# First slabs of a two-block transformer kernel: order of the first loads, gate logits as rounded products, and GpSimd's place in the opening

## The reference

```python
def hybrid_mixer(h, w_in, forget_b, ret_norm_g, w_out, valid):
    proj = jnp.einsum('bld,de->ble', h, w_in)
    rq, rk, rv, rg, fq, fk, fv, ff = jnp.split(proj, SPLIT_POINTS, axis=-1)
    o_r = retention(...)
    ...
    log_f = jax.nn.log_sigmoid(ff.astype(jnp.float32) + forget_b.astype(jnp.float32))
    o_f = forgetting_attention(fq..., fk..., fv..., log_f, valid)
    mixed = jnp.concatenate([o_r, o_f], axis=-1).astype(h.dtype)
    return jnp.einsum('ble,ed->bld', mixed, w_out)

def forgetting_attention(q, k, v, log_f, valid):
    c = jnp.cumsum(log_f, axis=1)           # logits get c[t] - c[s]
    ...
```

## Time and profile before

| | |
|---|---|
| median of 3 runs | 1465.71 us (1465.19 to 1465.89) |
| the profiled execution | 1465.56 us, span of the core 1463.8 us |
| TensorE busy | 1456.0 us, 99% of the span |
| VectorE / ScalarE / GpSimd busy | 902.1 / 768.0 / 490.2 us |
| HBM read | 247.79 MB |

### The profile page before, as it was taken

How to read it: one execution, slowest core, us unless ns; L and a number is a source line. 1 busy time by engine, 2 the same in 40 slices (tenths; PEclk the granted TensorE clock), 3 DMA queues, 4 the chain that set the end, 5 groups by cost and what they waited for, 6 DMA issues and landing times.

```text
span 1463.8 us, 30914 instructions
## 1 busy us (share of the span) xinstructions
PE 1456.0 (99%) x11461; PEld 1422.5 (97%) x11461; DVE 902.1 (62%) x1572; ACT 768.0 (52%) x1096; POOL 490.2 (33%) x209
## 2 busy tenths in 40 slices
PE   9999999999999999999999999999999999999998
PEld 7999999989999999999999999999999999999987
DVE  7437888755445369989644434544447898864533
ACT  6456655555445445567544534444444657654443
POOL 5541000443334303710244442443420570044442
PEclk9999999999999999999999999999999999999999
DMA  7435566655556545445555654555544535567763
GB/s 267 127 95 169 172 189 193 216 165 158 175 172 208 167 129 169 141 150 165 179 172 172 209 179 127 186 170 183 203 151 144 173 119 184 174 195 201 207 190 112
DMA packets 75882, 250.92 MB, mean 171 GB/s; under 512 B 15776, under 2 KB 18208, under 8 KB 75808
## 3 DMA queue, kind: packets, MB, share of 16 engines
q1 hardware_dynamic: 75280, 249.65, 54.6%
q10 hardware_dynamic: 528, 0.26, 0.1%
HBM read 247.79 MB, written 1.05 MB: 170 GB/s over the span
## 4 chain that ended last, share of the span: by engine, by line
PE 97%; DVE 1%; POOL 1%; issue 0%; DMA 0%; ACT 0%; SPq 0%; POOLq 0%; DVEq 0%
PE W L1645 27%; PE W L1646 27%; PE W L1647 27%; PE W L1733 3%; PE XP L1797 2%; PE XQ L1797 1%; PE W L1732 1%; PE W L1697 1%; PE W L1748 1%; PE W L1747 1%; PE W L1698 1%; PE W L1746 1%; PE W L1699 1%; DMA raw<-in_w 0%; POOL wlo L455 0%
## 5 line engine op out<-in xcount | busy, mean ns | idle before, releaser
L455 POOL TENSOR_TENSOR wlo<-raw,whi 128x1024 fp32r<-128x1024 f32 (+1 forms) x184 | 470.7, 2563 | 924.8 <-ACT whi L518 924.8
L1645 PE MATMUL W<-xh,whi 128*128 128x272 f32 (+2 forms) x2400 | 689.8, 287 | 0.2 <-POOL wlo L455 0.2
L1646 PE MATMUL W<-xl,whi 128*128 128x272 f32 (+2 forms) x2400 | 687.0, 286 | 0.0
L1647 PE MATMUL W<-xh,wlo 128*128 128x272 f32 (+2 forms) x2400 | 685.9, 286 | 0.0
L518 ACT ACTIVATE whi<-raw 128x1024 fp32r<-128x1024 f32 (+1 forms) x440 | 481.1, 1098 | 136.0 <-PE W L1647 94.1
L1645 PEld LDWEIGHTS W<-xh,whi 128*128 128x128 f32 x2400 | 452.4, 188 | 2.7 <-issue 1.5
L1647 PEld LDWEIGHTS W<-xh,wlo 128*128 128x128 f32 x2400 | 452.2, 188 | 0.0
L1646 PEld LDWEIGHTS W<-xl,whi 128*128 128x128 f32 x2400 | 451.3, 188 | 0.2
L986 DVE TENSOR_TENSOR wlo<-raw,whi 128x1024 fp32r<-128x1024 f32 (+1 forms) x255 | 331.9, 1302 | 80.1 <-ACT whi L518 79.7
L1645 PE MATMUL W<-ax,whi 128*128 128x272 f32 (+2 forms) x816 | 234.4, 287 | 0.1
L1647 PE MATMUL W<-ax,wlo 128*128 128x272 f32 (+2 forms) x816 | 234.3, 287 | 0.0
(11 more groups left out here) (280 smaller groups left out, 1399.9 us busy)
## 6 DMA issues: line engine op xcount, KB each, us to landing
raw<-in_w SPq DMA_DIRECT2D x377, 512.0 KB, 3.6
raw<-in_w SPq DMA_DIRECT2D x64, 704.0 KB, 4.1
h<-in_hT SPq DMA_DIRECT2D x4, 272.0 KB, 4.7
proj<-proj SPq DMA_DIRECT2D x16, 64.0 KB, 3.6
scr<-in_cst SPq DMA_DIRECT2D x1, 1000.0 KB, 9.5
out<-proj SPq DMA_DIRECT2D x3, 256.0 KB, 2.8
raw<-in_w SPq DMA_DIRECT2D x2, 256.0 KB, 3.6
proj<-in_gain SPq DMA_DIRECT2D x1, 512.0 KB, 4.5
```

Of the source, the lines that this page charges most:

```text
L455: pool.tensor_tensor(wlo[:, j, 0:cols], raw[:, j, 0:cols], whi[:, j, 0:cols].bitcast(F32), ALU.subtract).then_inc(lo_ready[j], 1)
L1645: pe.matmul(out, whi[:, j, w], mh, start=start and k == 0, stop=False, skip_group_check=True)
L1646: pe.matmul(out, whi[:, j, w], ml, start=False, stop=False, skip_group_check=True)
L1647: ins = pe.matmul(out, wlo[:, j, w], mh, start=False, stop=stop and k == len(rhs) - 1, skip_group_check=True)
```

## The change

- **Loads.** ScalarE's queue now issues the parameters `prm` and the first quarter of `h`; SyncE starts at once with the first half of slab 0, then the second quarter of `h`. The constants `cst1` (1000 KB) go behind the first slab of group 1, and `m2` and the late parameters behind all four of them.
- **Start.** The set-to-zero for the warm-up covers 272 instead of 512 columns, and WARM_UP is 5 instead of 4. The first half of slab 0 is rounded and subtracted in two quarters, each behind its chunk of `x`, the second half at m = 4 instead of m = 2.
- **Gates.** POOL rounds the gate weights (`wffr`, two parts) and TensorE makes each `forget_logits(k)` of three rounded products of `xh` and `xl`, all eight within the first slab; none is left at s = 2. VectorE's multiplication of gate weights by gain is gone.
- **POOL.** It takes over `lo(0, 2)` from VectorE, makes `lo(0, 2)`, `lo(0, 3)`, `lo(1, 0)` and `lo(1, 1)` first, waits for `ff_step` = 2 (line 1264's operation done), makes `lo(1, 2)`, and only then the casts and memsets, then `lo(1, 3)`, the last two casts, and the rest.
- Semaphores for late loads are merged (`late_landed`).

```diff
@@ sync
-            sp.dma_start(prm[:, 0:PRM_CW1], prm_d[:, 0:PRM_CW1]).then_inc(prm_landed, 16)
-            load_h(0)
-            load_half(0, 0)
-            load_half(0, 1)
+            load_part(0, S8 // 2, half_landed)
             load_h(1)
+            load_part(S8 // 2, S8, raw_landed[0])
             load_h(2)
             load_h(3)
...
+            sp.dma_start(cst[:, :], cst_d).then_inc(cst_landed, 16)
             sp.dma_start(fb_s, fbias).then_inc(fb_landed, 16)
-            sp.dma_start(cst[:, :], cst_d).then_inc(cst_landed, 16)
+            load(1, slab8(W8_QKV1 + 4), 0, S8)
             sp.dma_start(scr[:, 0:SC1_CONST], cst1_d).then_inc(c1_landed, 16)
+            for j in range(1, 4):
+                load(1, slab8(W8_QKV1 + 4 + j), j, S8)
...
@@ gpsimd
+            wff = prm[:, PRM_WFF:PRM_WFF + DC * FOX_H]
+            pool.wait_ge(prm_landed, 16)
+            pool.tensor_copy(wffr[:, 0, :], wff).then_inc(gate_step, 1)
+            pool.wait_ge(gate_step, 1)
+            pool.tensor_tensor(wffr[:, 1, :], wff, wffr[:, 0, :].bitcast(F32), ALU.subtract).then_inc(gate_step, 1)
+            lo(0, 2, S8)
             lo(0, 3, S8)
+            lo(1, 0, S8)
+            lo(1, 1, S8)
+            pool.wait_ge(ff_step, 2)
+            lo(1, 2, S8)
             pool.wait_ge(cst_landed, 16)
             pool.tensor_copy(identr[:, :], ident).then_inc(hide_ready, 1)
...
             pool.memset(proj[:, FQ:FK + 2 * CC - 1, 0:T_A], 0.0).then_inc(q_zero, 1)
+            lo(1, 3, S8)
             pool.wait_ge(c1_landed, 16)
...
-            los(N_QKV1 - 1, 1, K8A)
+            los(N_QKV1 - 2, 2, K8A)
@@ scalar
+            act.dma_start(prm[:, 0:PRM_CW1], prm_d[:, 0:PRM_CW1]).then_inc(prm_landed, 16)
+            act.dma_start(h[:, 0:2, :], hT[:, 0:2, :]).then_inc(h_landed[0], 16)
...
             for m in range(DC):
-                if m == 2:
-                    hi_part(0, 0)
+                if m == 4:
                     hi_part(0, 1)
                 act.wait_ge(h_landed[m // 2], 16)
                 split_x(0, m)
+                if m < 2:
+                    hi_quarter(m)
@@ vector
             lo_part(1, 1)
-            dve.wait_ge(hi_ready[2], 1)
-            dve.tensor_tensor(wlo[:, 2, 0:S8], raw[:, 2, 0:S8], whi[:, 2, 0:S8].bitcast(F32),
-                              ALU.subtract).then_inc(lo_ready[2], 1)
@@ tensor
             def forget_logits(k):
-                pe.wait_ge(wffg_ready, 1)
-                pe.wait_ge(h_landed[k // 2], 16)
-                return mm(X[2][0:FOX_H, 0:T], wffg[:, k, :], h[:, k, :], k == 0)
+                out, w = X[2][0:FOX_H, 0:T], slice(FOX_H * k, FOX_H * k + FOX_H)
+                mm(out, wffr[:, 0, w], xh[:, k, :], k == 0)
+                mm(out, wffr[:, 0, w], xl[:, k, :], False)
+                return mm(out, wffr[:, 1, w], xh[:, k, :], False)
...
                 if s == FORGET:
-                    forget_logits(6)
                     pe.wait_ge(cst_landed, 16)
                     stat(0)
-                    forget_logits(7).then_inc(ff_mm, 1)
```

More of the change, by code:

```diff
@@ L172 @@
 RET_S, RET_T, RET_V, RET_SUM = 17, 17, 18, 19
-WARM_UP = 4
+WARM_UP = 5
 FV, FQ, FK, RQ, RK, RV, RG = 0, 4, 5, 12, 14, 16, 20
@@ L209, in build @@
         selr, tailr = sb("selr", [P, FOX_H], F32R), sb("tailr", [P, P], F32R)
+        wffr = sb("wffr", [P, 2, DC * FOX_H], F32R)
         m2 = sb("m2", [P, DC, META])
@@ L286, in build @@
         half_landed = sem("half_landed")
-        hi_half, lo_half = sem("hi_half"), sem("lo_half")
+        hi_first, lo_first = sem("hi_first"), sem("lo_first")
         h_landed = [sem(f"h_landed{i}") for i in range(DC // 2)]
-        prm_landed, taps_landed, cst_landed, c1_landed, m2_landed = (
-            sem(x) for x in ("prm_landed", "taps_landed", "cst_landed", "c1_landed", "m2_landed"))
+        prm_landed, late_landed, cst_landed, c1_landed, m2_landed = (
+            sem(x) for x in ("prm_landed", "late_landed", "cst_landed", "c1_landed", "m2_landed"))
         fb_landed, q_zero, eps_set = sem("fb_landed"), sem("q_zero"), sem("eps_set")
-        wffg_ready, ff_mm, ff_step, ff_log, lt_mm, lf_ready, c_mm, c_ready = (
-            sem(x) for x in ("wffg_ready", "ff_mm", "ff_step", "ff_log", "lt_mm", "lf_ready", "c_mm", "c_ready"))
+        ff_mm, ff_step, ff_log, lt_mm, lf_ready, c_mm, c_ready = (
+            sem(x) for x in ("ff_mm", "ff_step", "ff_log", "lt_mm", "lf_ready", "c_mm", "c_ready"))
         vt_mm, vt_ready, rt_mm, rt_ready = (sem(x) for x in ("vt_mm", "vt_ready", "rt_mm", "rt_ready"))
-        mask_ready, sel_step, qz_zero, qz_ready, lf_zero = (
-            sem(x) for x in ("mask_ready", "sel_step", "qz_zero", "qz_ready", "lf_zero"))
+        mask_ready, gate_step, qz_zero, qz_ready, lf_zero = (
+            sem(x) for x in ("mask_ready", "gate_step", "qz_zero", "qz_ready", "lf_zero"))
         fl_mm, fl_max, fl_exp, fp_step, fp_ready, ft_mm, ft_ready, fo_mm, fo_hi, fo_lo, fl_step = (
@@ L383, in loads, with load_part @@
                         load(g + i, slab(first_slab + 4 * i + j), j, cols)
-            def load_half(j, half):
-                cols = slice(half * S8 // 2, (half + 1) * S8 // 2)
-                sp.dma_start(raw[:, j, cols], slab8(j)[:, cols]).then_inc(raw_landed[j] if half else half_landed, 16)
+            def load_part(a, e, landed):
+                sp.dma_start(raw[:, 0, a:e], slab8(0)[:, a:e]).then_inc(landed, 16)
             def load_h(i):
                 sp.dma_start(h[:, 2 * i:2 * i + 2, :], hT[:, 2 * i:2 * i + 2, :]).then_inc(h_landed[i], 16)
-            sp.dma_start(prm[:, 0:PRM_CW1], prm_d[:, 0:PRM_CW1]).then_inc(prm_landed, 16)
-            load_h(0)
-            load_half(0, 0)
-            load_half(0, 1)
+            load_part(0, S8 // 2, half_landed)
             load_h(1)
+            load_part(S8 // 2, S8, raw_landed[0])
             load_h(2)
@@ L475, in _ @@
             pool.tensor_copy(later_r[:, :], minus_later).then_inc(hide_ready, 1)
[L476 to L479, removed]
+            pool.tensor_copy(selr[:, :], ident[0:P, 0:FOX_H]).then_inc(gate_step, 1)
+            pool.wait_ge(gate_step, 3)
+            pool.tensor_copy(selr[FOX_LO, :], ident[FOX_LO, FOX_LO]).then_inc(gate_step, 1)
+            pool.wait_ge(gate_step, 4)
             pool.tensor_copy(tailr[:, :].rearrange("p (h q) -> p h q", h=FOX_H),
@@ L659, in first_out_proj, with hi_quarter @@
                 tail(7)
+            act.dma_start(prm[:, 0:PRM_CW1], prm_d[:, 0:PRM_CW1]).then_inc(prm_landed, 16)
+            act.dma_start(h[:, 0:2, :], hT[:, 0:2, :]).then_inc(h_landed[0], 16)
             act.preload_act_table_set("sqrt_and_others")
+            def hi_quarter(k):
+                cols = slice(k * S8 // 4, (k + 1) * S8 // 4)
+                act.wait_ge(half_landed, 16)
+                act.activation(whi[:, 0, cols], raw[:, 0, cols], ACT.Copy).then_inc(hi_first, 1)
             def hi_part(j, half):
                 cols = slice(half * S8 // 2, (half + 1) * S8 // 2)
[L665 to L669, removed]
+                act.wait_ge(raw_landed[j], 16)
+                act.activation(whi[:, j, cols], raw[:, j, cols], ACT.Copy).then_inc(hi_ready[j] if half else hi_first, 1)
             act.wait_ge(prm_landed, 16)
             for m in range(DC):
-                if m == 2:
-                    hi_part(0, 0)
+                if m == 4:
                     hi_part(0, 1)
@@ L1220, in first_out_proj @@
                 tail(7)
-            dve.memset(vT[:, 0, :], 0.0).then_inc(warm_set, 1)
+            dve.memset(vT[:, 0, 0:T], 0.0).then_inc(warm_set, 1)
             dve.memset(vT[:, 2, :], 0.0).then_inc(rest_zero, 1)
@@ L1226, in _, with lo_quarter @@
             dve.memset(s1("lf"), 0.0).then_inc(lf_zero, 1)
+            def lo_quarter(k):
+                cols = slice(k * S8 // 4, (k + 1) * S8 // 4)
+                dve.wait_ge(hi_first, k + 1)
+                dve.tensor_tensor(wlo[:, 0, cols], raw[:, 0, cols], whi[:, 0, cols].bitcast(F32),
+                                  ALU.subtract).then_inc(lo_first, 1)
             def lo_part(j, half):
@@ L1232, in lo_part @@
                 else:
-                    dve.wait_ge(hi_half, j + 1)
+                    dve.wait_ge(hi_first, 3)
                 dve.tensor_tensor(wlo[:, j, cols], raw[:, j, cols], whi[:, j, cols].bitcast(F32),
-                                  ALU.subtract).then_inc(lo_ready[j] if half else lo_half, 1)
+                                  ALU.subtract).then_inc(lo_ready[j] if half else lo_first, 1)
             dve.wait_ge(prm_landed, 16)
-            dve.tensor_tensor(wffg[:, :, :], wff_s[:, :, :],
-                              prm[:, PRM_G:PRM_G + DC].rearrange("p (k n) -> p k n", n=1).to_broadcast([P, DC, FOX_H]),
-                              ALU.mult).then_inc(wffg_ready, 1)
             for m in range(DC):
-                if m == 2:
-                    lo_part(0, 0)
+                if m == 4:
                     lo_part(0, 1)
```

(7 more changed lines are left out.)

28 lines of the change are left out of this document (14 added, 14 removed).

## The result

The changed kernel takes 1469.3 us (median of 15 runs, 1467.64 to 1470.72), the kernel before beside it 1465.75 us (15 runs, 1465.19 to 1466.15). The ratio is 1.0022, 95% interval 1.0016 to 1.0029: 3.5 us slower, above the forecast range of 1464.0 to 1468.8.

What follows compares the result with a forecast made beforehand. TensorE was taken to bound the kernel, running almost without a pause from 1.5 us on. 1.25 us won and 2.7 lost gave +1.45, 1467.0 us, within 0.2% (no change that can be told); range 1464.0 to 1468.8.

Steps and rivals of the forecast that it cites:

- the one on the clock: At TensorE's 2.7 us wait ahead of `fox_logits(0)`: granted clock stays at 1.00, so nothing counted for a slower clock.
- the sum: `fox_logits(0)` at 36.85 instead of 35.40: 1.25 us won, 2.7 lost, +1.45, giving 1467.0 us.
- Start of the first slab: TensorE's first product in the opening: starts at 6.3 (5.8 to 6.9) instead of 6.42.
- the landing: Arrival of the first quarter of `h`, ahead of the first slab: 4.7, the middle between 4.17 and 1.2 us later.
- TensorE's work: Opening up to `fox_logits(0)`: first slab 6.05 us with gate products, `stat` at 18.5, 1.25 us won if nobody is late.
- The port: VectorE against GpSimd on SBUF: line 1264 drops from 2.35 to about 0.25 us once GpSimd is kept off.
- This chain: From line 1264 through late memsets and `q_zero` (Z + 9.75) to line 1290's second cast, ending at Z + 18.35.
- a collision: Line 1290's casts wait for GpSimd subtractions ahead of `fox_logits(0)`: 2.7 us lost; stall of 1.5 to 3 us, 50%.
- the first: Rival at line 1290: no collision, or only the rest of one operation; 1464.3 or 1464.7 us; chance 35%.
- the second: Rival: line 1264 falls into `lo(1, 1)`, up to 2.4 us more, 1469.4; slip beyond 1.5 us, chance 10%.

Runs made afterwards that it cites:

- e6: Changed kernel with the `q_zero` memset at GpSimd's start and the first quarter of `h` at the head of SyncE's queue, ahead of the half slab: 1464.79 us.
- e1: The changed kernel again, unaltered: 1469.32 us, ratio 1.0024 to the kernel before; its profiled execution took 1470.57 us.
- e4: The changed kernel with two more warm-up products (`WARM_UP = 7`): 1468.62 us, ratio 1.0020 to the kernel before.
- e8: The kernel before with only GpSimd's new order of subtractions, casts and memsets: 1469.66 us, ratio 1.0021.
- e2: The changed kernel with the memset that releases `q_zero` made at GpSimd's start: 1465.79 us, ratio 1.0005 to the kernel before.
- e3: The changed kernel, `q_zero` still late, with GpSimd waiting for `c_ready` = 4 ahead of group 2's second subtraction: 1466.2 us, ratio 1.0005.
- e7: The changed kernel with GpSimd's old order, casts and memsets behind `lo(0, 3)` again: 1465.68 us, ratio 1.0000 to the kernel before.
- e11: The changed kernel with the `q_zero` memset at GpSimd's start, run a second time unaltered: 1465.62 us, ratio 0.9999 to the kernel before.
- e5: The changed kernel with the `q_zero` memset at GpSimd's start and eight warm-up products: 1465.89 us, ratio 1.0000 to the kernel before.
- e9: Changed kernel with zeros early, `h` first, and GpSimd waiting for the first pair's maxima ahead of group 2's third subtraction: 1463.89 us, ratio 0.9987.
- e10: The changed kernel with zeros early and `h` first, run again without a further edit: 1465.01 us, ratio 0.9994 to the kernel before.

## Why the prediction was wrong

The forecast was 1467.0 us and "within 0.2%"; it is 1469.3 and 0.22% slower. **The step that failed is the one on the clock: "TensorE stands still for 2.7 us there. [...] so I count nothing for a slower clock."** It rested on one case, the end of the trace, where the clock was still 1.00 for 4 us after the last product. One case gives no lower bound of such a delay. In the kernel before the clock falls in the window just behind the one that I read; in the changed kernel's profiled execution it falls sooner after its last product:

```profile
1462.00:1463.70 1.70, 0.00 (x0) 0.78 0.54 152
```

```profile
1460.00:1464.00 4.00, 0.00 (x0) 0.87 0.64 188
```

Read as full clock and then half, the first falls at 1462.95, 5.1 us behind the end of the last product; the second at 1462.96, 3.0 us behind. In the 1470.57 us run it falls, read in the same way, at 37.05, 2.0 us behind the end of the last product of s = 6 (35.10):

```profile
37.00:37.30 0.30, 0.00 (x0) 0.59 1.13 328
```

So a pause of 2.5 us was followed by half clock in some executions and not in others, and the sum should have held it with its chance: 11 of the 15 runs are 1.4 us or more above the lowest. That is +1.6 us of the 2.3 between 1467.0 and the measured 1469.3.

The other steps:
- **Start of the first slab.** Forecast 6.3, measured 7.01, just beyond its late bound of 6.9. The working from landing to start was right (1.6 estimated, 5.45 to 7.01 is 1.56); the term that was mis-sized is the landing, 4.7 for 5.45, where I took the middle although the full 1.2 us of the half slab's transfer was the reasoned price. The load was issued at 1.2 us in both kernels and landed 1.28 us later. The Trainium skill (DMA: Bandwidth & Descriptors, section "Issuing engines are not separate DMA queues") has loads of two queues interleave on the same engines; the row agrees, and with `h` first (e6) `xh` starts 1.42 us earlier. This is the other +0.7 us of the 2.3. Each of the two errors alone would have left the time inside the range, at 1467.7 and 1468.6.
- **TensorE's work.** The first slab takes 7.01 to 13.12, 6.11 (forecast 6.05). `stat` is at Z = 19.18 (18.5 forecast, all of it the start), s = 4 at Z + 3.62 (Z + 3.8) without a wait, `forget_sums` at Z + 10.47 (Z + 10.6).
- **The port.** Line 1264's operation took 0.35 us (0.25), ending at 24.16, Z + 4.98 (Z + 5.0), the last memset at 28.90, Z + 9.72 (Z + 9.75), the evacuation at Z + 9.76 (Z + 9.8), the casts start at Z + 14.44 (Z + 14.6) and end at Z + 18.21 (Z + 18.35). The wait is 2.5 (2.7), and `fox_logits(0)` is at Z + 18.31. This chain held to 0.2 us at every link.
- **That it is this chain** the experiments show from four sides: it comes with GpSimd's order alone, goes with the old order, goes with the zeros early, and shrinks to 0.3 us where only the second cast is let through.
- **The rivals.** There was a collision, so the first falls; line 1264 did not fall into `lo(1, 1)` (it starts at 23.81, just where that ends), so the second falls. That its time, 1469.4, is nearly the one measured is chance.
- **The sum.** In the short executions 0.71 won at `forget_sums`, 2.80 lost: +2.1 us, 1467.7. In three quarters of the executions (18 of 24, e1 with them) 1.4 us or more come on top, 1469.3. Profiles of such executions (e1, e4, e8) show the clock; for the others it is read from their times and average clocks. The changed kernel has the pause behind the warm-up too, so a few of the 18 may be due to that.

Open stay three things. One is what sets whether the clock falls in a given execution. One is 0.5 us that the best version loses: it is 1.99 us ahead of before at `fox_logits(0)` and 1.98 at `fox_logits(1)` (40.94 and 42.92), but 1.5 at the last product (1456.03 and 1457.54). The third is the executions 1.5 to 2.1 us above their fellows where there is no long pause at `fox_logits(0)`. All eight are among the 40 of e2, e3, e7 and e11, which have a pause of 1.0 to 1.3 us behind the warm-up; there are none in the 42 of e5, e6, e9 and e10, where it is filled or gone, and none in 103 of the kernel before, which has no such pause. That points at the pause. The half pace at the start lasting longer would fit the times and would not show in the average clock, but no trace has caught such an execution: it is argued, not shown.

## What to carry to other kernels

When helpers' work is moved on one engine, follow the small signal behind it: here a memset of 0.19 us came 8.9 us later, held VectorE's queue, and moved two short casts into the one stretch in which GpSimd had no gap. Check each short VectorE operation that TensorE waits for against what GpSimd runs at that moment, and keep GpSimd off it with a wait where its own work has slack. The stalls of 2.2 to 2.5 us here had two prices, the stall and in two executions of three a slower clock behind it. Price such a stall by all executions: the profiled one can be of the cheap group.

## What was not expected of the hardware

- The granted clock fell in or behind a pause of 2.2 to 2.5 us that followed 28 to 30 us of work without a gap: by their times in 11 of 15 and 7 of 9 executions of the changed kernel, 5 of 10 of e4 and 6 of 10 of e8. It fell 2.0 us into the pause in two profiles (e1, e8) and 1.6 us after TensorE was back at work in the third (e4). It stayed at half for 3.4 or 6.8 us, although TensorE was busy again.
- The granted clock reads 1.00 from the start of every trace, but the warm-up's products start 0.45 us apart, and from 5.40 on 0.23 in e5, where they last longest. The change came as late as the first slab in e10.
- An operation on 128x2 numbers waited out a whole GpSimd subtraction: 2.21 us for 0.16. The size of a VectorE operation was no guide to its cost there.
